# One modulation strip of a half and two of a quarter, and the first query and key products cut to match, in a two-block transformer kernel on one core

## The reference, cut to what matters

```python
c_act = jax.nn.silu(c)
mod = (c_act @ ada_w[l] + ada_b[l]).reshape(B, N_MOD, D)[:, :, None, :]   # ada_w: 2048 x 12288
shift_m, scale_m, gate_m, shift_f, scale_f, gate_f = [mod[:, i] for i in range(N_MOD)]
h = rmsnorm(x, norm_mix_g[l]) * (1.0 + scale_m) + shift_m
...
(p_q, p_k, p_v, p_g, p_gk, ...) = jnp.split(h @ w_in, idx, axis=-1)       # q, k: 1024 columns each
...
mn = rmsnorm_2(mem, mem_g); kv = mn @ w_mem_kv                            # for both layers of block two
```

## Time and profile before

| | |
|---|---|
| median of 3 runs | 2670.5 us (2669.82 to 2670.72) |
| the profiled execution's own time | 2669.16 us |
| its span | 2667.4 us |
| PE busy | 2621.8 us (98%) |
| DVE busy | 1770.1 us (66%) |
| ACT busy | 1237.7 us (46%) |
| mean granted clock of PE | 0.998 |

### The profile page before, as it was taken

One profiled execution on the slowest core, in us unless ns is written; L12 is line 12 of the kernel. 1 busy time (PEld: TensorE's weight loads), 2 busy tenths in 40 slices (PEclk: granted clock), 3 DMA queues, 4 the chain that ended last, 5 costly groups with the idle time before them and its releaser, 6 DMA issues.

```text
span 2667.4 us, 34585 instructions
## 1 busy us (share of the span) xinstructions
PE 2621.8 (98%) x14268; PEld 2256.8 (85%) x14268; DVE 1770.1 (66%) x2121; ACT 1237.7 (46%) x1689; POOL 13.1 (0%) x26
## 2 busy tenths in 40 slices
PE   8999999999999999999999999999999999999998
PEld 7899788888889888888888888888889898899987
DVE  7875797767576676666665544456676658766765
ACT  6445544443445534443433344445354545535554
POOL 0000000000000000000000000000000000000000
PEclk9999999999999999999999999999999999999999
DMA  9997717888686376477776555565555557654243
GB/s 353 361 369 230 261 55 260 309 286 291 209 271 143 124 270 234 158 251 253 247 230 229 194 189 190 189 201 181 186 169 199 176 181 236 214 178 142 96 159 125
DMA packets 335409, 573.53 MB, mean 215 GB/s; under 512 B 22415, under 2 KB 100551, under 8 KB 333976
## 3 DMA queue, kind: packets, MB, share of 16 engines
q1 hardware_dynamic: 332450, 560.45, 62.9%
q0 software_dynamic: 2368, 10.77, 1.2%
q10 hardware_dynamic: 438, 0.15, 0.0%
HBM read 567.11 MB, written 4.21 MB: 214 GB/s over the span
## 4 chain that ended last, share of the span: by engine, by line
PE 88%; DVE 6%; DMA 2%; ACT 2%; issue 1%; SPq 0%; ACTq 0%; DVEq 0%
PE tile_ps L1052 81%; PE misc_ps L1052 6%; DVE w_lo L2231 2%; DMA w_raw<-in_w_mem_kv 1%; ACT w_hi L1681 1%; PE misc_ps L1434 1%; DMA w_raw<-in_w_in 1%; PE misc_ps L1274 1%; DVE probs_t L2343 1%; DVE strip_wide L2343 1%; PE misc_ps L1533 0%; DVE probs_t L2323 0%; PE misc_ps L1171 0%; DVE mem_lo L2610 0%; DVE w_guest L2231 0%
## 5 line engine op out<-in xcount | busy, mean ns | idle before, releaser
L2231 DVE TENSOR_TENSOR w_lo<-w_raw,w_hi 128x1024 fp32r<-128x1024 f32 x840 | 991.2, 1222 | 722.3 <-ACT w_hi L1681 719.3
L1681 ACT ACTIVATE w_hi<-w_raw 128x1024 fp32r<-128x1024 f32 x840 | 842.8, 1051 | 1100.3 <-PE tile_ps L1052 1046.7
L1052 PE MATMUL tile_ps<-w_hi,h_both 128*128 128x512 f32 x3008 | 819.4, 391 | 5.5 <-DVE w_lo L2231 4.5
L1052 PEld LDWEIGHTS tile_ps<-w_hi,h_both 128*128 128x128 f32 x3008 | 560.8, 188 | 126.2 <-issue 8.3
L1052 PE MATMUL tile_ps<-h_both,w_hi 128*128 128x256 f32 (+1 forms) x2624 | 517.1, 313 | 7.3 <-DVE w_lo L2231 5.5
L1052 PE MATMUL tile_ps<-w_lo,h_both 128*128 128x512 f32 x1504 | 464.3, 389 | 0.0
L1052 PEld LDWEIGHTS tile_ps<-h_both,w_hi 128*128 128x128 f32 x2624 | 382.0, 192 | 39.2 <-DVE w_lo L2231 5.9
L1052 PE MATMUL tile_ps<-h_both,w_lo 128*128 128x256 f32 x1632 | 343.9, 283 | 0.0
L1052 PEld LDWEIGHTS tile_ps<-w_lo,h_both 128*128 128x128 f32 x1504 | 282.3, 188 | 59.2
L1052 PEld LDWEIGHTS tile_ps<-h_both,w_lo 128*128 128x128 f32 x1632 | 260.5, 192 | 0.1
L1052 PE MATMUL tile_ps<-w_hi,o_hi 128*128 128x512 f32 x512 | 161.0, 394 | 2.9 <-DVE o_lo L2545 2.5
(11 more groups left out here) (408 smaller groups left out, 2118.0 us busy)
## 6 DMA issues: line engine op xcount, KB each, us to landing
w_raw<-in_w_in SPq DMA_DIRECT2D x88, 1024.0 KB, 5.3
w_raw<-in_ffn_w_in SPq DMA_DIRECT2D x88, 1024.0 KB, 5.0
w_raw<-in_ada_w SPq DMA_DIRECT2D x80, 1024.0 KB, 5.1
w_raw<-in_w_out SPq DMA_DIRECT2D x48, 1024.0 KB, 5.1
w_raw<-in_ffn_w_down SPq DMA_DIRECT2D x44, 1024.0 KB, 5.2
w_raw<-in_b_w_in SPq DMA_DIRECT2D x33, 1024.0 KB, 5.3
w_raw<-in_a_w_in SPq DMA_DIRECT2D x32, 1024.0 KB, 5.4
w_raw<-in_w_kv SPq DMA_DIRECT2D x24, 1024.0 KB, 5.1
```

The lines of the kernel that those rows point to most:

```text
L1052: return nc.tensor.matmul(o, l, r, start=start, stop=stop, skip_group_check=True)
L1681: f(w_hi[CUT_IN.get(s_, s_ % 2)][:, hf], w_raw[r % 4][:, hf], ACT.Copy).then_inc(cut_hi, 1)
L2231: ins = v.tensor_tensor(w_lo[b][:, hf], w_raw[r % 4][:, hf], f32(w_hi[b][:, hf]), ALU.subtract)
```

## The change

1. Strip 0 becomes features 0 to 1023 (16 loads), strips 1 and 2 are 512 features each (8 loads each). `AFTER` is written anew. Before, 22 of the 32 strip loads go ahead of the first piece of `gla_qa`, after it 21.
2. `gla_qa` covers chunks 0 to 7 (4 pieces), `gla_ka` still chunks 0 to 11 (6 pieces, now by chunks first), `gla_qb` chunks 8 to 15 (4 pieces), `gla_kb` chunks 12 to 15 (2 pieces). 16 pieces in all, as before.
3. `strip_total` uses transposes of the 128x128 blocks instead of matmuls with a column, and `strip_mod` gains two reductions on DVE, each over 1024 (strip 0) or 512 elements.
4. Strip 0 is summed after piece 1 of `mem_v1` (before: after piece 0 of `mem_k1`); strip 1 after piece 0 of `gla_ka` (before: after piece 0 of `gla_qa`); strip 2 after piece 5 of `gla_ka` (before: piece 3).
5. `strip_mod(0)` and the first two `mix_low` stand on DVE behind the split of the last piece of `mem_v1`, so ahead of the split of the first piece of `gla_qa`. `mix_pair(0)` and `(1)` stand at the same place on ACT. The other pairs are placed anew.
6. The four stores wait for the end of `gla_ka`; `q_part` and `k_part` move to other addresses, and the wait for the stores moves to `gla_v`.

```diff
-STRIPS = ((0, 512), (512, 1024), (1536, 512))
+STRIPS = ((0, 1024), (1024, 512), (1536, 512))
...
-         "mem_v0": [[(0, 5)], [(0, 6)], [(0, 7)], [(1, 0), (1, 1)]],
-         "mem_k1": [[(1, 2)], [(1, 3), (1, 4)], [(1, 5)], [(1, 6), (1, 7)]],
-         "mem_v1": [[(1, 8)], [(1, 9), (1, 10)], [(1, 11)], [(1, 12), (1, 13)]],
-         "gla_qa": [[(1, 14), (1, 15)], [(2, 0)], [(2, 1)], [(2, 2)], [(2, 3)], [(2, 4)]],
-         "gla_ka": [[(2, 5)], [(2, 6)], [(2, 7)], [], [], []]}
+         "mem_v0": [[(0, 5)], [(0, 6)], [(0, 7)], [(0, 8), (0, 9)]],
+         "mem_k1": [[(0, 10)], [(0, 11)], [(0, 12)], [(0, 13), (0, 14)]],
+         "mem_v1": [[(0, 15)], [(1, 0), (1, 1)], [(1, 2)], [(1, 3), (1, 4)]],
+         "gla_qa": [[(1, 5)], [(1, 6), (1, 7)], [(2, 0)], [(2, 1)]],
+         "gla_ka": [[(2, 2)], [(2, 3), (2, 4)], [(2, 5)], [(2, 6)], [(2, 7)], []]}
...
-            Product("gla_qa", 2, 3, across=True), Product("gla_ka", 2, 3),
-            Product("gla_qb", 2, 1), Product("gla_kb", 2, 1), ...
+            Product("gla_qa", 2, 2, across=True), Product("gla_ka", 2, 3, across=True),
+            Product("gla_qb", 2, 2, across=True), Product("gla_kb", 2, 1), ...
...
-        q_part = at("q_part", BIG + 16 * KB, [P, 2, 4 * S])
-        k_part = at("k_part", BIG + 24 * KB, [P, 2, 4 * S])
+        q_part = at("q_part", OB + 16 * KB, [P, 2, 4 * S])
+        k_part = at("k_part", OB + 24 * KB, [P, 2, 4 * S])
...
-        strip_acc = [probs_t[:]..., strip_wide[:], probs_t[:]...]
+        strip_acc = [strip_wide[:], probs_t[:]..., strip_wide[:, 0:1024]]
...
+        def turned_strip(s, k):
+            return bank[2 + k if s else k]
...
             all_taken(pool, G["mem_v1"])
+            pool.wait_ge(piece_done, G["gla_ka"].p1)
...
             def strip_total(s):
                 pe.wait_ge(strip_step, strip_ops(s, 16 // strip_chunks(s) - 1) + strip_chunks(s))
-                if s == 2:
-                    pe.wait_ge(mod_ready, 1)
+                if s:
+                    pe.wait_ge(mod_ready, s)
+                else:
+                    pe.wait_ge(xt_out, DC // 2)
                 for b in range(2 * STRIPS[s][1] // P):
-                    last = mm(strip_sums(s, b), strip_acc[s][:, b * P:(b + 1) * P], ones[:, 0:1], True, True)
+                    last = nc.tensor.transpose(turned_strip(s, b // 4)[:, b % 4 * P:(b % 4 + 1) * P],
+                                               strip_acc[s][:, b * P:(b + 1) * P], ident)
...
-                    between=[lambda: strip_total(0)] + [lambda j=j: (turn_x(2 * j), turn_x(2 * j + 1)) for j in range(3)])
-            product("mem_v1", *h_mem, between=[lambda: (turn_x(6), turn_x(7))])
-            product("gla_qa", *h, chunk_ready=as_normed("mix"), between=[lambda: strip_total(1)])
-            product("gla_ka", *h, between=placed({3: lambda: strip_total(2)}))
+                    between=[None] + [lambda j=j: (turn_x(2 * j), turn_x(2 * j + 1)) for j in range(3)])
+            product("mem_v1", *h_mem, between=[lambda: (turn_x(6), turn_x(7)), lambda: strip_total(0)])
+            product("gla_qa", *h, chunk_ready=as_normed("mix"))
+            product("gla_ka", *h, chunk_ready=as_normed("mix"), between=placed({0: lambda: strip_total(1), 5: lambda: strip_total(2)}))
...  (ACT)
-                    between=[lambda: (x_leaves(6), x_leaves(7)), lambda: (mix_pair(0), mix_pair(1))])
-            product("gla_qa", ..., pre=stored),
-                    between=[lambda: (mix_pair(2), mix_pair(3)), lambda: (mix_pair(4), mix_pair(5))])
-            product("gla_ka", ..., between=placed({4: lambda: (mix_pair(6), mix_pair(7))}))
+                    between=placed({0: lambda: (x_leaves(6), x_leaves(7)), 2: lambda: (mix_pair(0), mix_pair(1))}))
+            product("gla_qa", ..., between=[lambda: (mix_pair(2), mix_pair(3))])
+            product("gla_ka", ..., between=placed({1: lambda: (mix_pair(4), mix_pair(5))}))
+            product("gla_qb", between=[lambda: (mix_pair(6), mix_pair(7))])
...  (DVE)
-                v.tensor_tensor(two(mod[:, 0:2 * DC]), two(src[:, 0:2 * DC]), two(vec("ada_b", 0, 2 * DC)), ALU.add)...
+                for part in range(2):
+                    turned_ = turned_strip(s, part) if s else misc_ps[part]
+                    own.wait(v.tensor_reduce(mod[:, part * DC + c0:part * DC + c1], in_chunks(turned_[:], c1 - c0), AX.X, ALU.add))
+                v.tensor_tensor(two(mod[:, 0:2 * DC]), two(mod[:, 0:2 * DC]), two(vec("ada_b", 0, 2 * DC)), ALU.add)...
...
-            product("mem_k1", between=[lambda: sums("mix"), lambda: strip_mod(0)])
-            product("mem_v1", between=[None, lambda: mix_lows(0, 2)])
+            product("mem_k1", between=[lambda: sums("mix")])
+            product("mem_v1", between=placed({2: lambda: (strip_mod(0), mix_lows(0, 2))}))
...
-            product("gla_qa", between=[lambda: (strip_mod(1), mix_lows(2, 4)), lambda: mix_lows(4, 6)])
-            product("gla_ka", between=placed({4: lambda: (strip_mod(2), mix_lows(6, 8))}))
+            product("gla_qa", between=[lambda: mix_lows(2, 4)])
+            product("gla_ka", between=placed({1: lambda: strip_mod(1), 2: lambda: mix_lows(4, 6)}))
+            product("gla_qb", with_part(...), between=[lambda: strip_mod(2), lambda: mix_lows(6, 8)])
```

More of the change, by code:

```diff
@@ L197 @@
 AFTER = {"mem_k0": [[(0, 1)], [(0, 2)], [(0, 3)], [(0, 4)]],
[3 rows of a table removed]
-         "gla_qa": [[(1, 14), (1, 15)], [(2, 0)], [(2, 1)], [(2, 2)], [(2, 3)], [(2, 4)]],
-         "gla_ka": [[(2, 5)], [(2, 6)], [(2, 7)], [], [], []]}
[3 rows of a table added]
+         "gla_qa": [[(1, 5)], [(1, 6), (1, 7)], [(2, 0)], [(2, 1)]],
+         "gla_ka": [[(2, 2)], [(2, 3), (2, 4)], [(2, 5)], [(2, 6)], [(2, 7)], []]}
 PRODUCTS = [Product("mem_k0", 1, 4), Product("mem_v0", 1, 4, mode="N"),
             Product("mem_k1", 1, 4), Product("mem_v1", 1, 4, mode="N"),
-            Product("gla_qa", 2, 3, across=True), Product("gla_ka", 2, 3),
-            Product("gla_qb", 2, 1), Product("gla_kb", 2, 1), Product("gla_gk", 1, 1, kc=16, width=P, dmas=2),
+            Product("gla_qa", 2, 2, across=True), Product("gla_ka", 2, 3, across=True),
+            Product("gla_qb", 2, 2, across=True), Product("gla_kb", 2, 1), Product("gla_gk", 1, 1, kc=16, width=P, dmas=2),
             Product("gla_v", 4, 4, mode="N", rider=2, flat=True),
@@ L666, in program @@
                "gla_qa": plain(w_in, W_Q), "gla_ka": plain(w_in, W_K),
-               "gla_qb": lambda i, tb, g, q: w_in[:, 12:16, W_Q + tb * NT:W_Q + (tb + 1) * NT],
+               "gla_qb": lambda i, tb, g, q: w_in[:, 8 + 4 * q:12 + 4 * q, W_Q + tb * NT:W_Q + (tb + 1) * NT],
                "gla_kb": lambda i, tb, g, q: w_in[:, 12:16, W_K + tb * NT:W_K + (tb + 1) * NT],
@@ L1918, in mix_pair @@
                     act.wait_ge(piece_done, G["mem_v0"].p1)
-                act.wait_ge(gain_ready, 1 if j < 2 else 2 if j < 6 else 3)
+                act.wait_ge(gain_ready, 1 if j < 4 else 2 if j < 6 else 3)
                 act.wait_ge(xt_out, j + 1)
@@ L1950, in _ @@
             product("mem_v1", copy_to(lambda i, tb, g: mem_v_out[:, 1]),
-                    between=[lambda: (x_leaves(6), x_leaves(7)), lambda: (mix_pair(0), mix_pair(1))])
-            stored = [(st_mkv, 64)]
-            product("gla_qa", copy_to(lambda i, tb, g: q_part[:, tb, :], scale=GLA_DK ** -0.5, pre=stored),
-                    between=[lambda: (mix_pair(2), mix_pair(3)), lambda: (mix_pair(4), mix_pair(5))])
-            product("gla_ka", copy_to(lambda i, tb, g: k_part[:, tb, :]), between=placed({4: lambda: (mix_pair(6), mix_pair(7))}))
-            product("gla_qb")
+                    between=placed({0: lambda: (x_leaves(6), x_leaves(7)), 2: lambda: (mix_pair(0), mix_pair(1))}))
+            product("gla_qa", copy_to(lambda i, tb, g: q_part[:, tb, :], scale=GLA_DK ** -0.5),
+                    between=[lambda: (mix_pair(2), mix_pair(3))])
+            product("gla_ka", copy_to(lambda i, tb, g: k_part[:, tb, :]), between=placed({1: lambda: (mix_pair(4), mix_pair(5))}))
+            product("gla_qb", between=[lambda: (mix_pair(6), mix_pair(7))])
             product("gla_kb")
@@ L1992, in decayed @@
                     f(decay[e % 2][:, 4 * c:4 * c + 4], bank[c].rearrange("p (a b) -> p a b", a=4), ACT.Exp).then_inc(gl_ex, 1)
-            product("gla_v", copy_to(columns(gla_v), pre=[(taken[t % 2], t // 2 + 1) for t in range(G["gla_kb"].t0, G["gla_kb"].t1)]),
+            product("gla_v", copy_to(columns(gla_v), pre=[(st_mkv, 64)] + [(taken[t % 2], t // 2 + 1) for t in range(G["gla_kb"].t0, G["gla_kb"].t1)]),
                     between=[None] + [lambda j=j: log_sigmoid(j) for j in range(4)] + [None] + [lambda j=j: log_high(j) for j in range(4)] +
@@ L2650, in with_part @@
                 return take
-            product("gla_qa", between=[lambda: (strip_mod(1), mix_lows(2, 4)), lambda: mix_lows(4, 6)])
-            product("gla_ka", between=placed({4: lambda: (strip_mod(2), mix_lows(6, 8))}))
```

(4 more changed lines are left out.)

7 lines of the change are left out of this document (3 added, 4 removed).

## The result

| | before | after |
|---|---|---|
| median of 20 runs each | 2669.85 us | 2673.58 us |
| lowest and highest | 2665.73 to 2671.88 | 2669.81 to 2676.69 |
| ratio, 95% interval | | 1.0012 [1.0007, 1.0018] |
| profiled execution: time, span | 2669.16, 2667.4 us | 2669.81, 2668.0 us |
| PE busy | 2621.8 us | 2615.0 us |

The change costs 3.7 us by the medians and 0.12% by the ratio, whose interval is 1.9 to 4.8 us. The profiled execution after is the shortest of its 20, so the two profiles differ by 0.65 us only. In the stage that the change touches they differ by 2.6 us, and that is where they are compared here. Of these, 0.5 us are there already when `mem_k1` starts (76.48 against 75.94).

What follows compares the result with a forecast made beforehand. Loads bound the kernel until about 153 us, then PE. Gains, stalls and clock losses put the fourteenth piece at 227.8 against 225.9: +1.9 us, 2671.1 by the profile, 2672.4 as median; range 2665.0 to 2677.0.

Steps and rivals of the forecast that it cites:

- The stall before the first query piece: PE idle from 130.4 until DVE's queue reaches that piece's split: 6.6 us, start at 137.0 instead of 133.74.
- The clock behind it: First query piece after the idle stretch runs partly at the lower clock: +1.7 us, 137.0 to 144.4.
- The waits before the fourth key piece and the third piece of `gla_qb`: PE waits 2.6 us in `gla_ka` behind ACT's two pairs, and 1.4 us after two query pieces in `gla_qb`.
- The clock behind the 2.6 us: Lower clock after the wait before the fourth key piece: +1.7 us; without it, -1.3 us on the sum.
- The wait of 1.3 us before the third query piece: PE done with the second query piece at 150.1, then waiting 1.3 us for DVE's split, done at 151.3.
- (a): One strip load fewer ahead of `gla_qa`: 1 MB less, 2.83 us of DMA time.
- (b): Stores, 2 MB, moved from 133.95 to beyond 200 us: 5.7 us of traffic, costed at nothing there.
- The reductions: DVE's added strip work: `strip_mod(0)` 2.8 us instead of 0.35, strips 1 and 2 1.7 us each.
- `T`: End of the last `gla_ka` piece on PE, put at 202.5 us; the last norm step is counted from it.
- The loads decide: Rival, chance 0.20: DVE keeps up, the tenth load comes 5.7 us earlier; -5.4 us, 2665.1 us.
- Nothing moves: Rival, chance 0.18: waits and strip sums that go pay for the 6.6 us wait; within 1 us of 2670.5.
- Slower by the clock in the last wait: Rival, chance 0.08: half clock for a whole piece after the 1.4 us wait in `gla_qb`; +5.8, 2678.1 us.

Runs made afterwards that it cites:

- Strip between: Changed kernel with strip load (1, 3) multiplied on DVE between `strip_mod(0)` and the low parts; 2670.97 us, ratio 1.0001 against the kernel before.
- low parts behind: Changed kernel with `strip_mod(0)`, the first pairs and low parts one step later, behind the first query piece's split; 2673.93 us, ratio 1.0014 against the kernel before.
- pairs late: Changed kernel with `mix_pair(4)`, `mix_pair(5)` and their low parts one step later in `gla_ka`; 2668.69 us, ratio 0.9999 against the kernel before.
- changed kernel again: The changed kernel unedited, timed beside the variants; 2673.89 us, ratio 1.0009 against the kernel before.
- stores early: Changed kernel with the four stores issued at their old time, behind `mem_v1`; 2678.32 us, ratio 1.0030 against the kernel before.
- filled wait: Changed kernel with twelve dummy matmuls of 512 columns on PE in the wait before the first query piece; 2672.76 us, ratio 1.0015 against the kernel before.
- three edits: Changed kernel with strip sums by one-column matmuls, strip load (1, 3) earlier on DVE, pairs 4 and 5 one step later; 2667.87 us, ratio 0.9992 against before.
- before with stores late: Kernel before with only the stores behind `gla_ka`, the new `q_part` and `k_part` addresses and the wait in `gla_v`; 2669.08 us, ratio 1.0000 against the kernel before.
- kernel before with transposed sums: Kernel before with only the strip sums changed to transposes plus two reductions on DVE; 2670.11 us, ratio 0.9999 against the kernel before.
- three edits with stores early: The three edits kernel with the stores issued at their old time; 2669.86 us, ratio 1.0000 against the kernel before.
- sums by columns: Changed kernel with the old strip sums, matmuls with a column of ones, and no reductions on DVE; 2668.45 us, ratio 0.9994 against the kernel before.

## Why the prediction was right, and where it was not

Forecast 2672.4 us (+1.9), measured 2673.58 (+3.7), inside the range of 2665.0 to 2677.0.

**The stall before the first query piece: right.** At 138.13, predicted 137.0; a wait of 7.50 us, predicted 6.6; ended by DVE's queue in the predicted order. Strip between shortens it and gains 2.9 us by the medians; low parts behind, which leaves DVE's queue as long (6.08 us of waiting), gains nothing. The 1.1 us too few were there before the stall: the split of `mem_v1`'s last piece ends at 123.3 instead of 122.4, and from there on the steps take what they were priced at (gain to low parts 4.40 against 4.35 us, strips 5.3 against 5.2). That `mem_k1` starts 0.5 us later than in the profile before is part of it.

**The clock behind it: right in kind, too small.** It is 0.50 from 136 to 140 and 0.63 from 140 to 144. The term was 1.7 us; with the wait filled the five pieces up to the strip sum take 2.1 us less. After every wait of 4.68 us and more the first four matmuls take 1.19 or 1.20 us (1.22 once), against 0.71 at 2.4 GHz.

**The waits before the fourth key piece and the third piece of `gla_qb`: right,** 2.61 and 1.40 for 2.6 and 1.4. That ACT's two pairs make the first is shown by pairs late: 0.51 us left, 3.8 us gained by the medians.

**The clock behind the 2.6 us: a toss, not a term.** It stays at 1.00 in three profiles with this wait (after, stores early, strip between) and is 0.66 to 0.70 over the next 5 us in three (again, low parts behind, filled wait). I had put in 1.7 us whole, because 2.6 lies nearer to 2.38 than to 1.55. A row of the kernel before that I didn't use speaks against that reasoning:

```profile
75.94 0.71 PE L1052 MATMUL tile_ps<-mem_hi,w_hi 128*128 128x256 f32 x4 [2.91 <-issue]
```

It is also a wait of PE that my list of its waits up to 153 us leaves out. Behind 2.91 us the matmuls take 0.71 us, and the clock is 1.00 over the next 5 us.

**That the profile came out so close: luck in part.** The fourth key piece starts at 185.17 instead of 183.5, because its low part and the steps before it follow a load that took 7.43 us. The clock that I had put in behind it, 1.7 us, isn't lost in this execution. Two errors of one size cancel, and the fourteenth piece is done at 228.5, forecast 227.8.

**The wait of 1.3 us before the third query piece: wrong.** There is none that the trace shows. The split ends at 151.6, as priced (151.3). But PE started 1.1 us later than I had it and lost more at the clock, and by my estimate comes to that piece at about 151.8, not at 150.1: 5.76 us a piece, counted back from the strip sum at 169.41, with a pause of 0.3 us at 157.5.

**"The 7.7 us of DMA time that (a) and (b) save go idle here": wrong for the stores.** This is the step that failed. The DMA engines do stand idle, at a share of 0.30, but early stores would have been issued only at 134.97, after that gap (stores early), and cost 4.4 us there. So the change's late stores aren't a part without effect. By the medians they pay for more than half of what its other parts cost: without them the change is at +7.7 us.

**The reductions: right one by one, too small together.** I costed 2.8 us in front of the first query piece, and 2.9 were measured (123.24 to 126.13), and the two others as parts of the chains behind `T`. What I didn't draw from it is that the old form would be 5.4 us better in this order (3.8 in the stage of the two profiles): all three times the reductions stand on DVE ahead of an operand that PE waits for, while PE's own saving of 1.7 us at the first sum falls into a wait and only 0.8 us at each of the others is left.

**Landing times: at the bound.** I took 5.3 to 6.5 us and named 7.4 as the other end; the chain shows 7.43 and 7.93.

**The size: about half.** +1.9 us was forecast; it is +2.6 us in the stage of the profiled pair, +3.3 and +3.7 in the medians. Between 1390 and 2301 us the profiled execution before loses 1.9 us that the one after doesn't; why is open. The 6 to 7 us from the lowest to the highest execution go with the clock: of the changed kernel again, the shortest (2671.05 us) has a mean granted clock of 0.997 and the longest (2676.38) one of 0.995.

**The rivals.** *The loads decide* falls as a forecast, but not wholly as a mechanism: early stores cost 4.4 us, and in that run the chain goes through a load of 11.63 us. The wait of 2.89 us that the three edits run into ends on DVE's strips; the load had landed 2.7 us before that split begins. *Nothing moves* lies outside the interval. *Slower by the clock in the last wait* falls: the clock isn't down behind the 1.40 us in any of the profiles read.

## What to carry to other kernels

Where one engine's queue makes both the operand that the bottleneck waits for and the release that lets loads go, count the queue in front of that operand: 5.3 us of multiplying that wasn't urgent stood ahead of it. In an exchange of work between two engines, price the two sides separately: here the 1.7 us that PE saved at the first sum fell into a wait of PE and bought nothing, while the reductions stood ahead of what PE waited for, and the exchange as a whole cost 5.4 us. In another order of the work it cost nothing that could be measured. Edits that shorten the same delay don't add up: -12.1 us alone, -5.6 together, and then PE waited for the next split behind two strips. And before a transfer is called free because the DMA engines are idle, look whether its issue falls into the gap or behind it.

## What the runs showed of the hardware

- Waits of one length are followed by either level of the clock. Over the 5 us behind it the granted clock was 1.00 after 3.34 us (stores early) and 0.50 after 2.89 us (three edits), 1.00 after 2.91 us (the kernel before, at 75.94), 1.00 or 0.66 to 0.70 after 2.62 us, and 0.66 after 1.73 us (before with stores late, at 155.03). After a wait of 2.07 us (pairs late, at 75.55) the first four matmuls took 1.19 us, as at 1.2 GHz. After 4.68 us and more (eight profiles with such a wait of PE) it was down every time, after 1.40 never.
- Sixteen transposes (1.91 us) left the clock at 1.00 between pieces (window 144 to 150 in the kernel before with transposed sums). The Trainium skill (TensorE: Matmul & The Clock Gate, Part 4) says that transposes don't count for the clock as matmuls do; in runs of this length no drop shows, here or over the 3 us behind the sixteen transposes in any of the other eight profiles that have them.
- Behind the 32 one-column matmuls of the wide strip's sum the clock was down in three of five profiles: 0.50 or 0.51 over 3 us in the kernel before, before with stores late and three edits with stores early, 1.00 in sums by columns and three edits. That the columns are the cause is likely beside the nine profiles with transposes, but it isn't shown.
- The twelve dummy matmuls of 512 columns took 10.46 us, two records and 0.87 us each, in the filled wait, at a clock of 1.00.
